# Eight key tiles are transposed and stored in the attention's last units instead of in the second value projection

## The chip, the cores and the metric

One NeuronCore of one Trainium2 chip runs the whole kernel. The metric is the device time of one execution in microseconds; lower is better. The engines are TensorE (PE in the rows), VectorE (DVE), ScalarE (ACT), GpSimd (POOL) and SyncE (SP), which here only issues DMAs.

## The reference

The kernel computes one inference step of a one-layer decoder for a prompt of 1024 tokens and 8 sampled tokens, each with a cache of 1024 positions in pages. Cut to what matters here:

```
h = rmsnorm(x); z = h @ w_in
gq, gk, gv, gr, g_lr, dq, dk, dv = split(z)
gla_o = chunked gated linear attention of gq, gk, gv
diff_o = (softmax(q1 k1^T) - lam * softmax(q2 k2^T)) @ v      # 4 heads, causal
x = x + concat(gla_o, diff_o) @ w_out
x = x + hier_moe(rmsnorm(x))                                   # 16 experts, top 2 of 4 in a group
return y, dk, dv, gla state                                    # dk of the prompt is an output: 1024 x 512
```

`dk` is the array that the change is about: the new keys are needed twice, with the head dimension on the partitions for the scores, and as rows by token, in float32, for the output `k_prompt`.

## The kernel before, in words

Every engine has a program of its own, written by hand in one order, and the engines meet at semaphores. Tokens go in tiles of 128 (NT = 8 tiles of the prompt, and a ninth of the 8 sampled tokens). PSUM has eight banks, `ps[:, 0]` to `ps[:, 7]`. The stages around the change are these, in order of time:

- **Key projection (DKG).** The keys are made transposed, as a high and a low float16 part, `kdh` and `kdl` (in `dg_reg`).
- **Second value projection (DVG).** PE makes the nine tiles of the values, 24 matmuls of 512 columns each (lines 2329 to 2331 of a shared helper, from `w_reg` and `hT_reg`), in banks 0 to 3. After each tile `between_values` runs `natural(n, t, hi, lo)`, eight matmuls against the identity that turn one tile of keys into rows by token in bank 4 or 5 (lines 2422 and 2423), and then one or two `value_quad(k)` (line 2548): a value quad multiplies four pages of the cached values, which SP has loaded into one of three buffers (`mix_reg`, or either half of `kv`), by the sampled tokens' weights. There are 16 quads, and 64 pages of 256 KB. SP reads each page's number from the page table (line 761) and then issues the load (line 762). ACT evicts each key tile to `knat` (line 1265, in `mix_reg`) and issues its store to `k_prompt` (line 1270); before the attention starts, ACT waits until all nine stores have landed (line 1274). The list `KNAT` puts the sampled tokens' keys first.
- **Attention.** UN = 32 units (8 tiles of queries times 4 heads, u = 0 to 31), followed by ten closing units u = 32 to 41 without scores of their own, in which the work behind the scores is finished. In unit u, PE transposes the combined weights (line 2633), multiplies by the values (line 2701), and does one quarter of an output product of an early tile (`early_product`, lines 2329 to 2331 from `w_reg` and `mix_reg`). `early_transpose(t, lo)` (line 2658, eight transposes into bank 4) puts one half of the normalised rows of tile t into bank 4, and ACT reads it away with line 1306 (`read_transposed`); PE may not write bank 4 again before that. `early_router` follows. ACT also squares the attention's output (line 1338), the new residual row (line 1289), rounds h2 (line 1354), and rounds the transposed attention output (line 649).
- **The product of tile 6** (`product(EARLY)`, 48 matmuls into banks 0 and 1) runs in unit 36, and the product of tile 7 (banks 2 and 3) after the closing units. Behind it come DVE's sum (line 2000), the norm, the router, and the experts. SP loads the first expert's weights when the stores of the early rows have landed and `s_h2T` says that tile 5 has been transposed:

```
            for i in range(2):
                sp.wait_ge(s_h2o[i], 16 * (EARLY // 2))
            sp.wait_ge(s_h2T, 2 * EARLY)
            load_gate_up(0)
```

Banks 2 and 3 hold scores up to unit 31 and nothing between that and the product of tile 7.

Of the kernel before, what the change touches and what calls it, by code (L numbers as in the profile page):

```python
# [98 lines left out]
KNAT = [NT] + list(range(NT))  # L99
# [62 lines left out]
def build(nc, I, O):  # L162
    ctx = ExitStack()
    with ctx:
# [125 lines left out]
        h2s = hT_reg[:, 4096:6144].bitcast(F16).rearrange("p (s d) -> p s d", s=2)  # L290
        h2T = hT_reg[:, 6144:8192].bitcast(F16).rearrange("p (s l k t) -> p s l k t", s=2, l=2, k=KC)
# [733 lines left out]
        def _(act):  # L1025
# [221 lines left out]
            for t in range(NT + 1):  # L1247
                r = rows(t)
                u = UNIT_AT[(DVG, t, 0)]
                if t in (3, 5):  # L1250
                    split_wo(t // 2 - 1)
                if t == NT - 1:
                    act.wait_ge(s_mT, NT + 1)
                    read_parts(DVG)
                if u % 2 == 0:
                    act.wait_ge(s_mm, u + 1)
                    act.activation(*plain_target(DVG, t, 0), ACT.Copy, scale=ISC2).then_inc(s_ev[BANK[u]], 1)
                v = KNAT[t]
                r = rows(v)
                act.wait_ge(s_kn, t + 2)  # L1260
                if t == 4:
                    act.wait_ge(s_dec, DEC["new_in"])
                if t >= 4:
                    act.wait_ge(s_kout[t % 4], 16 * (t // 4))
                act.activation(knat[0:r, t % 4], ps[0:r, 4 + (t + 1) % 2, :], ACT.Copy,
                               scale=1.0 / SC).then_inc(s_knr, 1)
                act.wait_ge(s_knr, t + 2)
                dst = O["k_prompt"][0, 0, v * P:(v + 1) * P].rearrange("p h e -> p (h e)") if v < NT \
                    else O["k_sample"][0, :, 0].rearrange("b h e -> b (h e)")
                act.dma_start(dst, knat[0:r, t % 4]).then_inc(s_kout[t % 4], 16)  # L1270
                if t == 4:
                    act.activation(dex, dex, ACT.Exp, scale=DK ** -0.5).then_inc(s_deca, 1)
            for i in range(4):
                act.wait_ge(s_kout[i], 16 * (NT // 4 + (i == 0)))
# [33 lines left out]
            for u in range(UN + 10):  # L1308
# [37 lines left out]
                if u % H == 1 and 0 <= (u - 17) // H < EARLY:  # L1346
                    t = (u - 17) // H
                    act.wait_ge(s_h2, t + 1)
                    if t == 0:
                        act.wait_ge(s_wol, KC // 2)  # L1350
                    if t >= 2:
                        act.wait_ge(s_h2o[t % 2], 16 * (t // 2))
                        act.wait_ge(s_h2T, 2 * (t - 1))
                    act.activation(h2se[:, t % 2, 0:D], h2e, ACT.Copy).then_inc(s_h2h, 1)
                if u == DEC_AT:
# [18 lines left out]

            for t in range(EARLY, NT + 2):
# [139 lines left out]
        def _(dve):  # L1515
# [502 lines left out]

            for t in range(EARLY, NT + 3):
# [306 lines left out]
        def _(pe):  # L2326
# [88 lines left out]
            def natural(n, t, hi, lo):  # L2415

                r = rows(t)
                if n >= 2:
                    pe.wait_ge(s_knr, n - 1)
                for h in range(H):  # L2420
                    out = ps[0:r, 4 + n % 2, P * h:P * h + P]
# [150 lines left out]
            def between_values(t, _):  # L2572
                natural(t + 1, KNAT[t], kdh, kdl)
                for k in QUADS_AT[t]:
                    value_quad(k)
# [42 lines left out]
            pe.wait_ge(s_knr, NT + 2)  # L2618
# [53 lines left out]
            for u in range(UN + 10):  # L2672
# [50 lines left out]
                if u % H == 1 and 0 <= (u - 21) // H < EARLY:  # L2723
                    early_router((u - 21) // H)
                if u == UN + 4:
                    product(EARLY)

            for t in range(EARLY + 1, NT + 3):
                if t == NT - 1:
                    product(t)  # L2730
# [210 lines left out]
```

## Time and profile before

| what | us |
|---|---|
| median of 3 runs | 917.7 (916.82 to 920.81) |
| the profiled execution, its own time | 914.89 |
| its span | 913.1 |
| PE busy in it | 788.1 (86%) |
| ACT busy in it | 444.9 (49%) |
| DVE busy in it | 561.8 (62%) |
| mean DMA rate over the span | 169 GB/s |

The difference of the last two times, 1.8 us, lies outside the span. All times of the rows below are from the span's start. A row of the timeline gives an instruction's start, its duration, the engine and the line; a matmul's duration is longer than the distance to the next one, since they are pipelined. `x8` means that eight alike were merged. In brackets stands for how long the engine was idle before, and what released it.

### The profile page before, as it was taken

How to read it: one execution, taken by the hardware profiler on the slowest of the kernel's cores; microseconds unless marked ns; L12 is line 12 of the kernel's file. 1: busy time of each engine (PE TensorE's matmuls, PEld its weight loads, DVE VectorE, ACT ScalarE, POOL GpSimd, SP SyncE). 2: the span in 40 equal slices, each digit the busy share in tenths (PEclk: the TensorE clock that was granted, in tenths of full speed). 3: DMA queues.
4: the chain of work that ended last, by engine and by line, in shares of the span. 5: the costliest groups of instructions: out<-in, count | busy, mean ns of one | idle time of the engine just before them, and what ended most of it. 6: DMA issues, size and time to landing. Idle time of an engine off the chain costs nothing. (4 is left out here: it accounts for less than half of the span.)

```text
span 913.1 us, 16430 instructions
## 1 busy us (share of the span) xinstructions
PE 788.1 (86%) x6255; PEld 494.6 (54%) x6255; DVE 561.8 (62%) x921; ACT 444.9 (49%) x855; POOL 249.2 (27%) x170
## 2 busy tenths in 40 slices
PE   3999979959899989976999998882389999998785
PEld 2766634335546644423566665441277787676551
DVE  6643569775444632248688875245675677787748
ACT  5432012557662412236467675234435757777733
POOL 2112987721134000002001000000424453532204
PEclk8999989979999999997999999986579999999998
DMA  9415795501031368881011101153596989999864
GB/s 310 102 50 151 234 300 183 194 0 47 1 99 47 93 224 256 258 279 69 25 70 70 71 24 47 47 209 129 190 312 222 293 259 302 304 338 342 233 207 186
DMA packets 98691, 154.70 MB, mean 169 GB/s; under 512 B 13573, under 2 KB 63301, under 8 KB 98610
## 3 DMA queue, kind: packets, MB, share of 16 engines
q1 hardware_dynamic: 91266, 132.97, 43.8%
q0 software_dynamic: 5728, 16.94, 7.3%
q10 hardware_dynamic: 1616, 3.70, 1.1%
q8 instruction: 51, 0.84, 0.4%
q14 instruction: 30, 0.25, 0.1%
HBM read 128.97 MB, written 27.48 MB: 171 GB/s over the span
## 5 line engine op out<-in xcount | busy, mean ns | idle before, releaser
L912 POOL TENSOR_TENSOR kv<-kv,gt 128x1024 f32<-128x1024 f32 x32 | 80.6, 2540 | 50.3 <-DMA kv<-in_cache_k 50.2
L2329 PE MATMUL ps<-hT_reg,w_reg 128*128 128x344 f16 x288 | 90.1, 313 | 3.5 <-DVE hT_reg L1564 3.5
L2330 PE MATMUL ps<-hT_reg,w_reg 128*128 128x344 f16 x288 | 89.9, 312 | 0.0
L2331 PE MATMUL ps<-hT_reg,w_reg 128*128 128x344 f16 x288 | 89.9, 312 | 0.0
L940 POOL TENSOR_TENSOR rst<-rst,neghalf 128x1 f32<-128x1 f32 (+3 forms) x27 | 24.8, 918 | 225.9 <-DVE rst L1861 225.9
L980 POOL DMA_INDIRECT sum_scratch<-kv,dest x23 | 59.4, 2583 | 89.9 <-DMA sum_scratch<-kv,dest 78.3
L2329 PE MATMUL ps<-w_reg,hT_reg 128*128 128x512 f16 x192 | 73.1, 381 | 1.9 <-ACT kv L1161 1.9
L2330 PE MATMUL ps<-w_reg,hT_reg 128*128 128x512 f16 x192 | 73.0, 380 | 0.0
L2331 PE MATMUL ps<-w_reg,hT_reg 128*128 128x512 f16 x192 | 72.9, 380 | 0.0
L1880 DVE TENSOR_REDUCE mxs<-ps 128x1 f32<-128x640 f32 (+7 forms) x48 | 45.7, 952 | 29.9 <-PE ps L2688 29.8
L2329 PE MATMUL ps<-hT_reg,dg_reg 128*128 128x128 f16 (+5 forms) x256 | 54.1, 238 | 2.0 <-DVE hT_reg L2157 2.0
L1320 ACT ACTIVATE hT_reg<-ps,mxn 128x128 f32<-128x128 f32 (+7 forms) x64 | 47.2, 740 | 17.7 <-DVE mxn L1881 11.5
L2329 PE MATMUL ps<-hT_reg,mix_reg 128*128 128x128 f16 (+4 forms) x256 | 52.9, 236 | 3.0 <-DVE hT_reg L2157 3.0
L1605 DVE TENSOR_REDUCE gbc<-kv 128x16 f32<-128x1024 f32 x32 | 38.8, 1215 | 26.2 <-POOL kv L912 26.2
L2330 PE MATMUL ps<-hT_reg,dg_reg 128*128 128x128 f16 (+5 forms) x256 | 54.1, 237 | 0.0
L2330 PE MATMUL ps<-hT_reg,mix_reg 128*128 128x128 f16 (+4 forms) x256 | 52.9, 236 | 0.0
L2331 PE MATMUL ps<-hT_reg,mix_reg 128*128 128x128 f16 (+4 forms) x256 | 52.8, 235 | 0.0
L2329 PE MATMUL ps<-w_reg,mix_reg 128*128 128x512 f16 x128 | 51.0, 399 | 0.0
L2331 PE MATMUL ps<-w_reg,mix_reg 128*128 128x512 f16 x128 | 50.7, 396 | 0.0
L2330 PE MATMUL ps<-w_reg,mix_reg 128*128 128x512 f16 x128 | 50.6, 396 | 0.0
L1298 ACT ACTIVATE hT_reg<-ps 128x512 f32<-128x512 f32 (+3 forms) x48 | 23.5, 489 | 45.0 <-PE ps L2633 44.1
L1579 DVE TENSOR_SCALAR dg_reg<-ps 128x512 f32<-128x512 f32 (+2 forms) x16 | 9.9, 616 | 54.7 <-PE ps L2331 45.0
(429 smaller groups left out, 2085.6 us busy)
## 6 DMA issues: line engine op xcount, KB each, us to landing
kv<-in_cache_k SPq DMA_DIRECT2D x64, 256.0 KB, 3.4
w_reg<-in_w_gate SPq DMA_DIRECT2D x16, 1024.0 KB
w_reg<-in_w_up SPq DMA_DIRECT2D x16, 1024.0 KB
w_reg<-in_w_down SPq DMA_DIRECT2D x16, 1024.0 KB, 14.8
w_reg<-in_w_in SPq DMA_DIRECT2D x12, 1024.0 KB, 6.6
mix_reg<-in_cache_v SPq DMA_DIRECT2D x32, 256.0 KB, 3.0
kv<-in_cache_v SPq DMA_DIRECT2D x32, 256.0 KB, 3.0
mix_reg<-in_x_prompt SPq DMA_DIRECT2D x8, 512.0 KB, 8.5
```

What stands on the lines that cost most here:

```text
L912: pool.tensor_tensor(pg, pg, qbc[:, b % 2].unsqueeze(1).to_broadcast([P, 2, 512]), ALU.mult).then_inc(s_kq, 1)
L940: pool.tensor_tensor(rst[pr, cr], rst[pr, cr], neghalf[pr, cr], ALU.pow).then_inc(s_rs, 1)
L980: pool.indirect_dma_start(out=sumd[:, :], out_offset=bass.IndirectOffsetOnAxis(ap=dest[0:r, 2 * e + g:2 * e + g + 1], axis=0), in_=yb[0:r, ...
L1298: act.activation(wT[:, v % 2, 4 * f:4 * f + w], ps[:, 4, 0:P * w].rearrange("p (j q) -> p j q", j=w), ACT.Copy).then_inc(s_wTe, 1)
L1320: act.activation(prob[:, u % 3, m, 0:n], scores(u, m), ACT.Exp, scale=DK ** -0.5 * ISC2, bias=mxn[:, u % 2, m:m + 1], accum_out=rsum[:, i ...
L1579: dve.tensor_scalar(*plain_target(g, blk, j), plain_scale(g, blk), None, ALU.mult).then_inc(s_ev[BANK[u]], 1)
L1605: dve.tensor_reduce(dsc[:, b, 2 * s:2 * s + 2], kv4[:, s].rearrange("p (g m d) -> p g m d", g=2, m=8), AX, ALU.add).then_inc(s_kh, 1)
L1880: link(dve.tensor_reduce(mxs[:, u % 2, ms], sc, AX, ALU.max))
L2329: pe.matmul(out, lh, rh, start=start, stop=False)
L2330: pe.matmul(out, lh, rl, start=False, stop=False)
L2331: return pe.matmul(out, ll, rh, start=False, stop=stop)
```

## The change

The eight prompt tiles' `natural` calls leave the second value projection and go to the end of the closing units u = 32 to 39, one in each, behind that unit's other PE work; the sampled tokens' call stays. They write banks 2 and 3. ACT's eviction and the store that follows go to the end of ACT's part of the same units; the eviction writes `keys_out`, a part of `hT_reg` that held attention weights and is used again for h2 afterwards. ACT waits for the stores to land before the loop that writes h2 there, not before the attention. PE waits that the keys are read before the product of tile 7, and DVE that they are transposed before it writes `x1` over `kdh` and `kdl`.

```diff
@@ ACT, second value projection
-                v = KNAT[t]
-                act.wait_ge(s_kn, t + 2)
+                if t == 0:
+                    act.wait_ge(s_kn, 2)
+                    act.activation(knat[0:NB, 0], ps[0:NB, 5, :], ACT.Copy, scale=1.0 / SC).then_inc(s_knr, 1)
+                    act.wait_ge(s_knr, 2)
+                    act.dma_start(O["k_sample"][0, :, 0].rearrange("b h e -> b (h e)"), knat[0:NB, 0]
+                                  ).then_inc(s_kout[0], 16)
                 if t == 4:
                     act.wait_ge(s_dec, DEC["new_in"])
-                if t >= 4:
-                    act.wait_ge(s_kout[t % 4], 16 * (t // 4))
-                act.activation(knat[0:r, t % 4], ps[0:r, 4 + (t + 1) % 2, :], ACT.Copy,
-                               scale=1.0 / SC).then_inc(s_knr, 1)
-                act.wait_ge(s_knr, t + 2)
...
-                act.dma_start(dst, knat[0:r, t % 4]).then_inc(s_kout[t % 4], 16)
...
-            for i in range(4):
-                act.wait_ge(s_kout[i], 16 * (NT // 4 + (i == 0)))
+            act.wait_ge(s_kout[0], 16)
@@ ACT, attention loop, end of unit u
+                if 0 <= u - UN < NT:
+                    t = u - UN
+                    act.wait_ge(s_kn, t + 3)
+                    if t >= 4:
+                        act.wait_ge(s_kout[t % 4], 16 * (1 + (t == 4)))
+                    act.activation(keys_out[:, t % 4], ps[:, 2 + t % 2, :], ACT.Copy, scale=1.0 / SC).then_inc(s_knr, 1)
+                    act.wait_ge(s_knr, t + 3)
+                    act.dma_start(O["k_prompt"][0, 0, t * P:(t + 1) * P].rearrange("p h e -> p (h e)"),
+                                  keys_out[:, t % 4]).then_inc(s_kout[t % 4], 16)
@@ ACT, before the loop over the last tiles
+            for i in range(4):
+                act.wait_ge(s_kout[i], 16 * (2 + (i == 0)))
@@ DVE, at the same place
+            dve.wait_ge(s_kn, NT + 2)
@@ PE
-            def natural(n, t, hi, lo):
+            def natural(n, t, hi, lo, bank=4):
...
-                    pe.wait_ge(s_knr, n - 1)
+                    pe.wait_ge(s_knr, n - 1 if n > 3 else 2)
...
-                natural(t + 1, KNAT[t], kdh, kdl)
+                if t == 0:
+                    natural(1, NT, kdh, kdl)
...
-            pe.wait_ge(s_knr, NT + 2)
+            pe.wait_ge(s_knr, 2)
@@ PE, attention loop, end of unit u, ahead of the product of tile 6
+                if 0 <= u - UN < NT:
+                    pe.wait_ge(s_p, 2 * UN)
+                    natural(u - UN + 2, u - UN, kdh, kdl, 2)
@@ PE, before the product of tile 7
+                    pe.wait_ge(s_knr, NT + 2)
```

In the changed kernel the lines are shifted: before's 2422 and 2423 are 2427 and 2428, 2658 is 2664, 2548 is 2553, 1306 is 1299, 1338 is 1331, 1289 is 1282, 1354 is 1347, and the keys' eviction and store are 1353 and 1355.

PE in the second value projection, at the end of one value tile; before:

```order
L2330 MATMUL ps<-w_reg,hT_reg 128x512
L2331 MATMUL ps<-w_reg,hT_reg 128x512
L2422 MATMUL ps<-ident,dg_reg 128x128
L2423 MATMUL ps<-ident,dg_reg 128x128
...
L2548 MATMUL ps<-kv,gbc 8x512 x4
L2329 MATMUL ps<-w_reg,hT_reg 128x512
```

and now:

```order
L2335 MATMUL ps<-w_reg,hT_reg 128x512
L2336 MATMUL ps<-w_reg,hT_reg 128x512
L2553 MATMUL ps<-kv,gbc 8x512 x4
L2334 MATMUL ps<-w_reg,hT_reg 128x512
L2335 MATMUL ps<-w_reg,hT_reg 128x512
```

The eight identity matmuls between the value tile and the value quad are gone, here and at seven more such places.

ACT in the closing units, from the squares of unit 35 on; before:

```order
L649 ACTIVATE mix_reg<-ps 128x4x128
L1338 ACTIVATE junk,ss<-ps,rinv 128x128 x2
L1289 ACTIVATE junk,ss<-kv 128x1024
L1306 ACTIVATE kv<-ps 128x1024
L1338 ACTIVATE junk,ss<-ps,rinv 128x128 x2
L1306 ACTIVATE kv<-ps 128x1024
```

and now:

```order
L649 ACTIVATE mix_reg<-ps 128x4x128
L1353 ACTIVATE hT_reg<-ps 128x512
L1355 DMA out_k_prompt<-hT_reg 128x512
L1331 ACTIVATE junk,ss<-ps,rinv 128x128 x2
L1282 ACTIVATE junk,ss<-kv 128x1024
L1353 ACTIVATE hT_reg<-ps 128x512
L1355 DMA out_k_prompt<-hT_reg 128x512
L1299 ACTIVATE kv<-ps 128x1024
L1331 ACTIVATE junk,ss<-ps,rinv 128x128 x2
L1353 ACTIVATE hT_reg<-ps 128x512
L1355 DMA out_k_prompt<-hT_reg 128x512
L1299 ACTIVATE kv<-ps 128x1024
```

An eviction and an issue of the keys now stand ahead of each of ACT's reads of the transposed h2.

PE at the same place, from the end of tile 5's output product to the product of tile 6; before:

```order
L2330 MATMUL ps<-w_reg,mix_reg 128x512
L2331 MATMUL ps<-w_reg,mix_reg 128x512
L2658 MATMUL ps<-ident,w_reg 128x128 x16
L2329 MATMUL ps<-w_reg,mix_reg 128x512
L2330 MATMUL ps<-w_reg,mix_reg 128x512
```

and now:

```order
L2336 MATMUL ps<-w_reg,mix_reg 128x512
L2427 MATMUL ps<-ident,dg_reg 128x128
L2428 MATMUL ps<-ident,dg_reg 128x128
...
L2664 MATMUL ps<-ident,w_reg 128x128 x8
L2427 MATMUL ps<-ident,dg_reg 128x128
...
L2664 MATMUL ps<-ident,w_reg 128x128 x8
L2427 MATMUL ps<-ident,dg_reg 128x128
...
L2334 MATMUL ps<-w_reg,mix_reg 128x512
```

Three of the moved key tiles stand around the two halves of h2's transposition of tile 4.

## Rows read from the trace of the kernel before

**Rows 1.** The page's head: the span.

```profile
span 913.1 us, 16430 instructions
```

**Rows 2.** Timeline of PE in the second value projection.

```profile
345.18 0.22 PE L2422 MATMUL ps<-ident,dg_reg 128*128 128x128 f16 x1
...
345.72 1.04 PE L2548 MATMUL ps<-kv,gbc 128*8 128x512 f32 x8
...
354.23 1.04 PE L2548 MATMUL ps<-mix_reg,gbc 128*8 128x512 f32 x8 [0.75 <-DMA mix_reg<-in_cache_v]
...
396.26 1.04 PE L2548 MATMUL ps<-mix_reg,gbc 128*8 128x512 f32 x8 [1.43 <-DMA mix_reg<-in_cache_v]
```

**Rows 3.** Timeline of SP's queue in the same stage: single issues of pages.

```profile
337.33 0.33 SPq L762 DMA_DIRECT2D kv<-in_cache_v  x1
...
347.55 1.04 SPq L762 DMA_DIRECT2D mix_reg<-in_cache_v  x1
...
362.90 0.33 SPq L762 DMA_DIRECT2D mix_reg<-in_cache_v  x1
364.64 0.33 SPq L762 DMA_DIRECT2D mix_reg<-in_cache_v  x1
...
392.43 0.33 SPq L762 DMA_DIRECT2D mix_reg<-in_cache_v  x1
```

**Rows 4.** Lines 761 and 762 over the whole span, ns (landing in us): minimum, median, maximum.

```profile
L761 SPq TENSOR_LOAD <-ptab x64: 262/268/920, 295.0 to 391.7; - x64
...
DMA to landing us min/median/max: 2.4/3.0/4.4
```

**Rows 5.** Timeline of ACT in the stage, with the issues of its queue (ACTq).

```profile
346.50 0.37 ACTq L1270 DMA_DIRECT2D out_k_prompt<-mix_reg  x1
...
352.54 0.60 ACT L1265 ACTIVATE mix_reg<-ps 128x512 f32<-128x512 f32 x1 [6.07 <-PE ps L2423]
...
353.63 1.91 ACT L1244 ACTIVATE w_reg<-w_reg 128x2048 f16<-128x2048 f32 x1 [0.49 <-ACT mix_reg L1265]
...
399.28 0.37 ACT L1320 ACTIVATE hT_reg<-ps,mxn 128x128 f32<-128x128 f32 x1 [4.79 <-DMA out_k_prompt<-mix_reg]
```

**Rows 6.** Timeline of PE at the attention's start.

```profile
399.78 1.88 PE L2710 MATMUL ps<-kv,lsel 128*8 128x512 f32 x4 [1.49 <-DVE kv L1943]
```

**Rows 7.** Timeline of PE in the closing units.

```profile
563.87 0.61 PE L2658 MATMUL ps<-ident,w_reg 128*128 128x128 f16 x8
565.79 0.63 PE L2633 MATMUL ps<-ident,hT_reg 128*128 128x128 f32 x4 [1.31 <-ACT kv L1306]
...
576.57 0.61 PE L2658 MATMUL ps<-ident,w_reg 128*128 128x128 f16 x8
579.88 0.61 PE L2658 MATMUL ps<-ident,w_reg 128*128 128x128 f16 x8 [2.70 <-ACT kv L1306]
...
596.51 0.61 PE L2658 MATMUL ps<-ident,w_reg 128*128 128x128 f16 x8 [1.31 <-ACT kv L1306]
```

**Rows 8.** Timeline of ACT in the closing units.

```profile
564.51 1.02 ACT L1306 ACTIVATE kv<-ps 128x1024 f16<-128x1024 f16 x1 [1.74 <-PE ps L2658]
...
577.57 1.06 ACT L1289 ACTIVATE junk<-kv 128x1024 f32<-128x1024 f32 x1 [2.10 <-DVE kv L1889]
...
578.62 1.00 ACT L1306 ACTIVATE kv<-ps 128x1024 f16<-128x1024 f16 x1
579.53 0.36 ACT L1338 ACTIVATE junk<-ps,rinv 128x128 f32<-128x128 f32 x1
...
580.52 1.02 ACT L1306 ACTIVATE kv<-ps 128x1024 f16<-128x1024 f16 x1 [0.20 <-PE ps L2658]
```

**Rows 9.** The chain that ended last, around the product of tile 7.

```profile
594.56 2.94 DMA h_scratch<-w_reg
...
612.06 1.29 DVE dg_reg L2000 x2
```

**Rows 10.** One window: length, busy time of PE, PEld, DVE, ACT, POOL, then granted clock, DMA share, GB/s.

```profile
600.00:620.00 20.00, 17.02 (x117) 7.29 (x115) 8.34 (x11) 8.76 (x12) 1.10 (x2) 0.88 0.45 160
```

More of the change, by code:

```diff
@@ L98 @@
 KCH = 4 * NB
-KNAT = [NT] + list(range(NT))
 VQ = 2 * NPG
@@ L290, in build @@
         h2s = hT_reg[:, 4096:6144].bitcast(F16).rearrange("p (s d) -> p s d", s=2)
+        keys_out = hT_reg[:, 4096:6144].rearrange("p (s c) -> p s c", s=4)
         h2T = hT_reg[:, 6144:8192].bitcast(F16).rearrange("p (s l k t) -> p s l k t", s=2, l=2, k=KC)
@@ L1257, in _ @@
                     act.activation(*plain_target(DVG, t, 0), ACT.Copy, scale=ISC2).then_inc(s_ev[BANK[u]], 1)
-                v = KNAT[t]
-                r = rows(v)
-                act.wait_ge(s_kn, t + 2)
+                if t == 0:
[4 more added lines that the diff above has]
+                                  ).then_inc(s_kout[0], 16)
                 if t == 4:
                     act.wait_ge(s_dec, DEC["new_in"])
-                if t >= 4:
-                    act.wait_ge(s_kout[t % 4], 16 * (t // 4))
-                act.activation(knat[0:r, t % 4], ps[0:r, 4 + (t + 1) % 2, :], ACT.Copy,
-                               scale=1.0 / SC).then_inc(s_knr, 1)
-                act.wait_ge(s_knr, t + 2)
-                dst = O["k_prompt"][0, 0, v * P:(v + 1) * P].rearrange("p h e -> p (h e)") if v < NT \
-                    else O["k_sample"][0, :, 0].rearrange("b h e -> b (h e)")
-                act.dma_start(dst, knat[0:r, t % 4]).then_inc(s_kout[t % 4], 16)
-                if t == 4:
                     act.activation(dex, dex, ACT.Exp, scale=DK ** -0.5).then_inc(s_deca, 1)
-            for i in range(4):
-                act.wait_ge(s_kout[i], 16 * (NT // 4 + (i == 0)))
+            act.wait_ge(s_kout[0], 16)
             squared = [0, 0]
@@ L2413, in next_x @@
                     x_transpose(t)
-            def natural(n, t, hi, lo):
+            def natural(n, t, hi, lo, bank=4):
                 r = rows(t)
                 if n >= 2:
-                    pe.wait_ge(s_knr, n - 1)
+                    pe.wait_ge(s_knr, n - 1 if n > 3 else 2)
                 for h in range(H):
-                    out = ps[0:r, 4 + n % 2, P * h:P * h + P]
+                    out = ps[0:r, bank + n % 2, P * h:P * h + P]
                     pe.matmul(out, hi[:, h, span(t)], ident16[:], start=True, stop=False)
```

## The prediction

> **What bounds the kernel now.** The page's head gives the span, 913.1 us [rows 1]; the profiled execution's own time is 914.89, and the median of the runs is 917.7, so 2.8 lies between my base and the number to be forecast. PE is busy for 86% of the span, but what the change is worth is decided at two places, and I read each by its timelines: first who waits, then for what.
>
> In the second value projection PE looks like the bound: it runs without a break but for three short waits, and each wait is for pages of cached values. Two stand in [rows 2], 0.75 us at 354.23 and 1.43 at 396.26, the last value quad, behind which the attention begins. So two chains end there almost together, PE's and SP's. SP issues the 48 pages of quads 4 to 15 from 337.33 to 392.43 [rows 3]; most of the 47 distances are 1.08 to 1.13 us, of which only 0.33 is the issue; the median read of the page number is 0.27 [rows 4] and the rest of the 1.09 is register work. 47 x 1.09 is 51.2, the rows give 55.1: 3.9 us are stalls. Two stand in [rows 3]: the issue at 347.55 took 1.04 instead of 0.33, and between 362.90 and 364.64 lies 1.74 instead of 1.09, for a page-number read that took up to 920 ns [rows 4]. In no place is SP held by PE: each buffer had been freed before SP asked.
>
> In the closing units PE is the bound, and wherever it stops it stops for ACT's read of bank 4: 1.31 at 565.79, 2.70 at 579.88, 1.31 at 596.51 [rows 7]. There ACT is the second half of a serial chain, not a spare engine.
>
> **Step 1, what leaves the value projection.** One call of `natural` is eight matmuls, and PE spends from 345.18 to 345.62 on it: 0.44 us (345.72 less the 0.10 before a quad) [rows 2]. Eight of them are 3.5 us. By PE alone that would be the gain. But the last quad starts when its pages land, 396.26, 1.43 us after PE was ready. If SP's stream stays as it is, PE only waits 3.5 us longer, and the gain is nothing, or at most 0.8: the last page took 3.8 us from its issue at 392.43 to 396.26, against a median of 3.0 [rows 3, 4], and one key store was on its way beside it.
>
> If the stalls go with the stores, the stream ends earlier. The first of the eight stores is issued at 346.50 [rows 5]; the stalled page issue at 347.55 begins 1.05 behind it. Each of the five long stalls of the stream follows a store by 0.9 to 1.7 us, and ahead of the first store there is only a short one of 0.36. The five sum to about 3.0. I take them as caused by the stores. Then the last page is issued at 389.5 and lands at 392.5 to 393.3. PE, freed of 3.5 us and of most of the wait at 354.23, is ready at about 390.7, so the pages still end the stage. Gain: 396.26 less 392.9, **3.3 us** (bounds 0 and 4.2, the second being 3.5 plus the 0.75 wait).
>
> The Trainium skill (Perfetto Trace Analysis, DMA Instruction — HWDGE) says that the block which writes the descriptors is shared by the issuing sequencers and locked, and that the reported issue includes the wait for the lock. By that rule eight stores of some 0.36 us could take at most 2.9 from SP. The stalled issue agrees; the long page-number reads are not explained by it.
>
> **Step 2, the wait ahead of the attention.** ACT's first exponential waits for the last store until 399.28 [rows 5]. That wait goes. It is worth nothing: PE has 1.88 us of work from 399.78 on that waits for DVE [rows 6], and it hides the exponentials. At no cover it would be 0.6.
>
> **Step 3, unit 32 to 33.** From here on all is the cost. In the rows of before PE's transposes at 563.87 end their turn at 564.31. Now `natural` follows, to 564.75, its last result some 0.2 later, and ACT, in its own order, has to evict the keys before it may read bank 4. What an eviction with its store costs ACT: 352.54 to 353.63, **1.09 us** [rows 5] (activation 0.60, then the issue, 0.37, for which ACT waits on its own result). So the read that began at 564.51 [rows 8] begins at 566.03, and PE goes on at 567.31 instead of 565.79: **+1.5**. Nothing hides it; PE is the stage's bound.
>
> **Step 4, units 33 to 36.** The key tiles of units 33 and 34 add 0.44 each to PE: transposition of tile 4 starts at +2.40, 578.97 instead of 576.57 [rows 7]. Before, ACT came to its read of the first half at 578.62, behind the square at 577.57 [rows 8]. Now it evicts tile 2 (579.2 to 580.26), does unit 35's two squares (579.53 to 580.32, 0.8) and the row's square (577.57 to 578.62, 1.05) to 582.15 [rows 8], evicts tile 3 (to 583.22), reads bank 4 (1.26 to PE's start, as from 578.62 to 579.88), and PE's second half starts at 584.48 instead of 579.88: **+4.6**, 2.2 more. Behind it stands tile 4's 0.44: the product of tile 6 starts at **+5.0**. ACT's keys of units 36 and 37 lie beside that product, 12 us, and cost nothing.
>
> **Step 5, units 37 to 41.** Counted from T, the start of tile 7's transposes (592.97 before, 3.54 ahead of the row at 596.51), PE does tile 5 (0.44), the transposes, tile 6 and, after DVE's h2 part, which arrives when it did before, the first half of tile 5's h2 at T + 1.62, then key tile 7. ACT has the keys at T + 0.67, its rounding at T + 1.73, then two evictions in a row, T + 2.22 to T + 4.35, and only then the read of bank 4, which before began at T + 2.26. So PE's second half comes at T + 5.62 instead of T + 3.54 (596.51 [rows 7]): **+2.1** for the product of tile 7. The same +2.1 stops `s_h2T`, which now releases the first expert's load: before, the store of 594.56 landed at 597.5 and released it [rows 9], now the transposes do, 1.65 later. Both meet at DVE's sum at 612.06 [rows 9]: about **+1.8** there. The cost is 5.0 + 1.8 = **6.8 us**. Its bounds: if the issue were free to ACT (0.49 an eviction, the distance of two activations), the same sum gives 4.5; if a store's landing held ACT once (3.7 us after the last issue at T + 3.95, ahead of ACT's next work at T + 9.8) nothing is added.
>
> **Step 6, the clock.** The window from 600 to 620 shows a granted clock of 0.88 [rows 10]: a stretch at the lower level, 1.2 instead of 2.4 GHz, follows the idle time of the closing units, and there is a shorter one behind the 2.70 idle at 579.88. The change makes two idle times longer, 1.31 to 2.6 and 2.70 to 4.6. Whether the first now brings a stretch at the low level of its own is open. The window's 12% of 20 us, twice, is a stretch of 4.8 us and cost half of it, 2.4; I take such a cost at less than even chance, **+0.9**. The bounds are 0 and +4.8, two more of them.
>
> The sum is 6.8 - 3.3 + 0.9 = **+4.4**: 919.3 in the profile's terms, 922.1 beside the median.
>
> **Rivals.** (a) SP's stalls are not the stores' doing and the stream ends as before. For it: three of the eight stores have no long stall behind them. The gain is 0 to 0.8: +6.9 to +7.7, 924.6 to 925.4. (b) The kernel is not slower, because the key matmuls keep PE active in the gaps: both low stretches go, the one in [rows 10], 2.4, and the one behind 579.88, at most as much. It gives 6.8 - 3.3 - 4.8 = -1.3, 916.4. It decides if the products of tiles 6 and 7 run every matmul at the full clock. Against it: a key tile fills 0.44 while the gap it stands in grows by 1.3 or more. The Trainium skill (TensorE: Matmul & The Clock Gate, HAM oscillation) holds that idle gaps bring the low clock back; longer gaps speak against this change by it. (c) The clock costs one stretch more, 2.4, or two: 6.8 - 3.3 + 2.4 = +5.9, 923.6, up to 926.0. (d) ACT's cost is the lower one: 4.5 - 3.3 + 0.9 = +2.1, 919.8.
>
> **How the numbers follow.** My forecast has 0.43, (a) 0.25, (b) 0.10, (c) 0.10, (d) 0.12. About 0.5%, 4.6 us, is what a measurement of this kernel can tell from no change, so the line is 922.3. Half of the forecast's own spread, 920 to 924, lies over it: slower by more is 0.21 + 0.25 + 0.10 = 0.56 less a little of (a), 0.53; faster by more than 0.5% is half of (b), 0.05; the rest, 0.42, is between. The range leaves out most of (b), the bottom of (d) and the top of (c): 918.8 to 926.0.
>
> **What would show it.** In the changed trace: the distances of SP's page issues all near 1.09 and the last quad before 393.5 (step 1; near 396 means (a)). PE's wait for bank 4 of 2.6 us at unit 33, 4.6 at unit 36 and about 3.1 and 1.5 in units 40 and 41, the excess each time taken by ACT's 1353 with 1.09 from its start to the next activation. The sum of step 4, read from value projection's end to the product of tile 6, is wrong if ACT got to the keys in a time when it had nothing else. The forecast fails if PE's low-clock stretches move by more than one, or if the experts' loads, which now start later, meet other traffic.

## The result, and the profile after

The changed kernel takes 924.1 us (median of 7 runs, 921.21 to 928.12) against 917.7 (7 runs, 914.2 to 920.81) on the same chip: a ratio of 1.0084, 95% interval 1.0055 to 1.0114. Slower, by 6.4 us in the medians; +4.4 was forecast. The ratio on record is not the quotient of the two medians (1.0070); here and below it leaves out runs in a slower state, among them one of e (3882.9 us) and one of f (1058.3). By it the change costs 7.7 us, with an interval of 5.0 to 10.5, and the forecast's 4.4 lies just under that interval. The profiled execution has its own time of 921.7 and this span, which answers to [rows 1]:

```profile
span 919.9 us, 16438 instructions
```

6.8 us more than before. I follow the two traces from front to back.

**Ahead of the stream.** The stream of pages begins 2.0 us later than in [rows 3], at 339.33. This has no part in the change: up to there both kernels run the same instructions. A window of the changed one shows a granted clock of 0.83 (length, busy time of PE, PEld, DVE, ACT, POOL, clock, DMA share, GB/s) where the same work before ran at 1.00; that is 0.5 us of it, and the other 1.5 come in between 195 and 199 us. The second trace of the changed kernel (h, below) begins its stream at 336.77, earlier than before. So the 2.0 are one execution's chance, and below I count from the stream's start.

```profile
160.00:170.00 10.00, 8.04 (x48) 2.81 (x46) 8.20 (x10) 0.60 (x1) 6.67 (x3) 0.83 0.81 259
```

**The value projection.** SP's first and last page issue of quads 4 to 15, and the reads of page numbers over the span (minimum, median, maximum in ns), to be held against [rows 3, 4]:

```profile
339.33 0.33 SPq L762 DMA_DIRECT2D kv<-in_cache_v  x1
...
391.47 0.33 SPq L762 DMA_DIRECT2D mix_reg<-in_cache_v  x1
```

```profile
L761 SPq TENSOR_LOAD <-ptab x64: 264/268/288, 297.0 to 390.8; - x64
```

The stream is 52.14 long instead of 55.10, and the longest read of a page number is 288 ns, not 920: the stalls are gone with the stores. PE's timeline at the end of the stage and the start of the attention ([rows 2, 6]):

```profile
394.96 1.04 PE L2553 MATMUL ps<-mix_reg,gbc 128*8 128x512 f32 x8 [2.60 <-DMA mix_reg<-in_cache_v]
398.48 3.58 PE L2716 MATMUL ps<-kv,lsel 128*8 128x512 f32 x4 [1.32 <-DVE kv L1947]
```

The last quad starts 55.63 us after the stream instead of 58.93: the 3.3 us of the forecast. But PE now waits 2.60 for its pages instead of 1.43, and the four matmuls of the second row take 3.58 instead of 1.88. Two windows from the last quad to unit 19's early transposes, the same work in both kernels, show what came of that:

```profile
396.26:475.65 79.39, 67.13 (x460) 36.95 (x461) 61.22 (x142) 45.17 (x137) 9.20 (x9) 0.94 0.27 99
```

```profile
394.96:476.19 81.23, 69.55 (x460) 37.52 (x461) 61.22 (x142) 45.18 (x137) 9.20 (x9) 0.89 0.26 94
```

The first is before, the second after: 1.84 us longer at a clock of 0.89 instead of 0.94. More than half of the 3.3 is lost again there. The lower clock falls right behind the last quad; again before, then after:

```profile
396.00:404.00 8.00, 5.36 (x48) 1.97 (x48) 4.55 (x15) 2.70 (x13) 0.00 (x0) 1.00 1.04 363
```

```profile
396.00:404.00 8.00, 6.36 (x38) 1.80 (x37) 3.89 (x14) 2.30 (x12) 0.00 (x0) 0.57 1.00 348
```

**The closing units**, PE's timeline, to be held against [rows 7]:

```profile
567.82 0.63 PE L2639 MATMUL ps<-ident,hT_reg 128*128 128x128 f32 x4 [2.35 <-ACT kv L1299]
...
585.01 1.01 PE L2664 MATMUL ps<-ident,w_reg 128*128 128x128 f16 x8 [4.50 <-ACT kv L1299]
...
603.72 0.61 PE L2664 MATMUL ps<-ident,w_reg 128*128 128x128 f16 x8 [2.89 <-ACT kv L1299]
```

The waits for bank 4 grew from 1.31, 2.70 and 1.31 to 2.35, 4.50 and 2.89. ACT's timeline shows what stands in front of its read of bank 4, which ends them. For the wait of 4.50 it is tile 3's eviction and its issue, and tile 2's was ahead of them:

```profile
582.69 0.58 ACT L1353 ACTIVATE hT_reg<-ps 128x512 f32<-128x512 f32 x1
583.30 0.34 ACTq L1355 DMA_DIRECT2D out_k_prompt<-hT_reg  x1
583.74 1.02 ACT L1299 ACTIVATE kv<-ps 128x1024 f16<-128x1024 f16 x1 [0.47 <-ACT hT_reg L1353]
```

and for the wait of 2.89:

```profile
600.31 0.59 ACT L1353 ACTIVATE hT_reg<-ps 128x512 f32<-128x512 f32 x1
600.93 0.34 ACTq L1355 DMA_DIRECT2D out_k_prompt<-hT_reg  x1
601.37 0.60 ACT L1353 ACTIVATE hT_reg<-ps 128x512 f32<-128x512 f32 x1 [0.47 <-ACT hT_reg L1353]
602.00 0.34 ACTq L1355 DMA_DIRECT2D out_k_prompt<-hT_reg  x1
602.44 1.02 ACT L1299 ACTIVATE kv<-ps 128x1024 f16<-128x1024 f16 x1 [0.47 <-ACT hT_reg L1353]
```

Two evictions, 1.06 us from start to start, then the read of bank 4 that PE waits for. The chain that ended last goes on from there ([rows 9]):

```profile
603.72 0.62 PE ps L2664 x8
604.41 0.38 SPq L781
604.84 10.81 DMA w_reg<-in_w_up
615.68 1.92 ACT dg_reg L1370
617.65 2.17 issue
619.83 1.29 DVE dg_reg L2004 x2
```

DVE's sum, line 2004 now, starts at 619.83 instead of 612.06. Of these 7.77 us 0.54 had come in before unit 32; 7.2 are the closing units' and the load's. Behind it the routing, at a lower clock for somewhat longer than before, adds about 1.0, and the experts give 1.9 back. Neither needs the change as its cause: from DVE's sum to the end all twelve traces of this document have the same work, and take 298.9 (f) to 304.1 us (g) for it. So 2.0 - 3.3 + 1.8 + 7.2 + 1.0 - 1.9 = 6.8, the difference of the spans.

### The profile page after: what moved, and what is told of

Its sections match the earlier page's. It is cut to its first block and busy times, and to the rows that moved or that the text cites. A ratio compares the mean times of both kernels' runs of the same rounds, so it can differ in the third digit from the quotient of the medians.

```text
span 919.9 us, 16438 instructions
## 1 busy us (share of the span) xinstructions
PE 794.0 (86%) x6255; PEld 497.1 (54%) x6255; DVE 561.7 (61%) x921; ACT 445.2 (48%) x855; POOL 252.4 (27%) x170
## 5 line engine op out<-in xcount | busy, mean ns | idle before, releaser
L980 POOL DMA_INDIRECT sum_scratch<-kv,dest x23 | 61.8, 2686 | 86.9 <-DMA sum_scratch<-kv,dest 75.4
L2334 PE MATMUL ps<-w_reg,mix_reg 128*128 128x512 f16 x128 | 50.4, 394 | 0.0
L2335 PE MATMUL ps<-w_reg,mix_reg 128*128 128x512 f16 x128 | 50.1, 391 | 0.0
L2336 PE MATMUL ps<-w_reg,mix_reg 128*128 128x512 f16 x128 | 49.9, 390 | 0.0
```

What stands on the lines that cost most here:

```text
L980: pool.indirect_dma_start(out=sumd[:, :], out_offset=bass.IndirectOffsetOnAxis(ap=dest[0:r, 2 * e + g:2 * e + g + 1], axis=0), in_=yb[0:r, ...
L2334: pe.matmul(out, lh, rh, start=start, stop=False)
L2335: pe.matmul(out, lh, rl, start=False, stop=False)
L2336: return pe.matmul(out, ll, rh, start=False, stop=stop)
```

## The experiments

Ten runs were made, one of them the changed kernel once more. Three questions were open: did the stores cause SP's stalls; is the closing units' cost ACT's evictions and nothing else; and what do the pieces give by themselves, so that a better place can be found. Ratios are to the kernel before on the same chip, with 95% intervals; they differ from the quotients of the medians by up to 0.25%. The code cuts show the lines that matter and leave out the semaphore waits that go with them. The columns behind come from each run's profiled execution: the length of SP's stream of quads 4 to 15; the time from the last quad to unit 19's early transposes with the granted clock of that window; the time from unit 32's early transposes to the product of tile 7.

| kernel | median us | ratio | stream | last quad to unit 19, clock | closing units |
|---|---|---|---|---|---|
| before | 917.7 | | 55.10 | 79.39, 0.94 | 35.19 |
| changed | 924.1 | 1.0084 [1.0055, 1.0114] | 52.14 | 81.23, 0.89 | 41.86 |
| a_no_stores | 914.71 | 0.9961 [0.9936, 0.9987] | 53.44 | 79.39, 0.94 | 35.20 |
| b_no_transposes | 915.66 | 0.9994 [0.9961, 1.0027] | 57.23 | 83.49, 0.87 | 33.51 |
| c_no_keys | 912.26 | 0.9947 [0.9917, 0.9978] | 52.99 | 79.94, 0.89 | 35.20 |
| d_no_issue | 919.4 | 1.0034 [1.0009, 1.0058] | 53.88 | 80.63, 0.92 | 40.73 |
| e_late_reads | 917.9 | 1.0013 [0.9985, 1.0041] | 52.38 | 81.52, 0.90 | 34.29 |
| f_first_units | 916.72 | 0.9991 [0.9970, 1.0011] | 52.48 | 83.23, 0.90 | 35.20 |
| g_pe_only | 915.66 | 0.9987 [0.9961, 1.0014] | 52.26 | 81.21, 0.89 | 34.38 |
| h_changed_again | 926.32 | 1.0110 [1.0077, 1.0143] | 52.54 | 82.62, 0.88 | 45.39 |
| i_late_no_stores | 912.04 | 0.9941 [0.9921, 0.9962] | 52.53 | 81.65, 0.90 | 34.00 |
| j_split_places | 915.9 | 0.9989 [0.9965, 1.0013] | 52.24 | 81.83, 0.92 | 34.21 |

a to d shared a chip (before: 916.1), e to h another (916.02), i and j a third (917.92).

### a_no_stores: the kernel before without the eight stores

```
                 act.activation(knat[0:r, t % 4], ps[0:r, 4 + (t + 1) % 2, :], ...)
-                act.wait_ge(s_knr, t + 2)
-                act.dma_start(dst, knat[0:r, t % 4]).then_inc(s_kout[t % 4], 16)
+                if t == 0:
+                    act.wait_ge(s_knr, 2)
+                    act.dma_start(dst, knat[0:r, 0]).then_inc(s_kout[0], 16)
```

> The kernel before, with the eight stores of the prompt's keys left out (k_prompt is not written; transposes and evictions stay). My theory: the stores cause SP's long stalls, so the stream of the 48 pages of quads 4 to 15 takes about 52 us from the first issue to the last instead of 55.1, and as PE still has its 3.5 us of key transposes, PE and pages end together: the last value quad comes 2.5 to 3.0 us earlier against the stage's start, and the whole is about 2.5 faster than before, less what the clock takes. Rival (a): the stream still takes 55 and the last quad is where it was; no change in time.

SP's reads of page numbers are at most 281 ns:

```profile
L761 SPq TENSOR_LOAD <-ptab x64: 263/268/281, 298.1 to 393.1; - x64
```

The stream shrinks by 1.7, and PE, which still makes the transposes, waits no more than 0.2 for the last quad. The stage's gain from the stores alone is 2.0 (56.89 from the stream's start to the last quad instead of 58.93), because PE is then the bound; I had expected 2.5 to 3.0, and a stream of 52 instead of 53.44. The whole is 3.6 us faster by the ratio, and its interval holds the 2.5 expected.

### b_no_transposes: the kernel before without PE's transposes, stores kept

```
             def between_values(t, _):
-                natural(t + 1, KNAT[t], kdh, kdl)
+                if t == 0:
+                    natural(1, NT, kdh, kdl)
```

ACT's eight evictions are left out too; it stores what the slots hold.

> The kernel before, with PE's and ACT's work on the eight prompt key tiles left out and the eight stores kept (they store what is in the buffer, so k_prompt is wrong). My theory: the stores still stall SP, the stream takes 55 us, the last quad starts when its pages land as before, and PE merely waits 3 to 4.5 us for it instead of 1.43; no gain (within 1 us). Rival (PE is the stage's bound): the last quad comes 3.5 us earlier, 3.5 faster.

The stream is not shorter but 2.1 longer: seven reads of a page number took 640 to 1164 ns, each 1.0 to 1.6 us behind the issue of a store. The row of line 761, and one page's issue, 2.65 us behind the first store:

```profile
L761 SPq TENSOR_LOAD <-ptab x64: 263/268/1164, 294.2 to 392.7; - x64
```

```profile
347.21 1.33 SPq L762 DMA_DIRECT2D mix_reg<-in_cache_v  x1
```

So PE's 3.5 us are worth nothing while the stores stay, as step 1 had it; and with PE idle for 4.26 us ahead of the last quad, the attention's start ran at a clock of 0.52:

```profile
397.92 1.90 PE L2549 MATMUL ps<-mix_reg,gbc 128*8 128x512 f32 x8 [4.26 <-DMA mix_reg<-in_cache_v]
```

```profile
396.00:404.00 8.00, 4.86 (x26) 1.10 (x27) 2.92 (x9) 1.62 (x8) 0.00 (x0) 0.52 0.94 321
```

### c_no_keys: the changed kernel without the eight key tiles

```
-                if 0 <= u - UN < NT:
-                    pe.wait_ge(s_p, 2 * UN)
-                    natural(u - UN + 2, u - UN, kdh, kdl, 2)
```

and ACT's part, so that the prompt's keys are missing from the output.

> The changed kernel with the eight prompt key tiles left out altogether (k_prompt is not written). It is the change's gain alone. My theory: the stage's end comes 3.3 us earlier as in the changed kernel, the closing units are as in before, the low-clock stretch at the attention's start costs about 1.8 of it: 1.5 to 3.3 faster than before, and 7 to 8 faster than the changed kernel. Rival: the closing units' delay comes from the earlier start or the clock and not from the keys; then it stays within 2 us of the changed kernel.

0.9947, 4.9 us by the ratio: this is what taking the tiles out of the value projection is worth if they cost nothing elsewhere. That is more than the 1.5 to 3.3 expected, though the interval, 2.0 to 7.6 us, reaches into it. The closing units are those of before to 0.01 us. The changed kernel's 1.0084 to 1.0110 lies 1.4 to 1.6% above it, 12.5 to 15 us, where I had expected 7 to 8; the profiled spans (910.1 and 919.9, less the 2.7 us by which the stream begins later in the changed trace) show 7.1. The rival, less than 2, is out by either.

### d_no_issue: the changed kernel, evictions kept, stores left out

```
                     act.activation(keys_out[:, t % 4], ps[:, 2 + t % 2, :], ...)
-                    act.wait_ge(s_knr, t + 3)
-                    act.dma_start(O["k_prompt"]..., keys_out[:, t % 4]).then_inc(s_kout[t % 4], 16)
```

> The changed kernel with the stores left out, transposes and evictions in the closing units kept (k_prompt is not written). My theory: an eviction then costs ACT 0.5 instead of 1.09 us. PE's idle time before the row that waits for bank 4 in unit 33 falls from 2.35 to about 1.8, in unit 36 from 4.50 to about 3.3, in unit 40 from 2.89 to about 1.2, and the load of the first expert's weights is released about 3.3 us earlier relative to unit 32: 2.5 to 3.5 us faster than the changed kernel, still 2 to 4 slower than before. Rival: the issue costs nothing, the evictions alone make the delay; same as the changed kernel.

```profile
564.50 0.63 PE L2632 MATMUL ps<-ident,hT_reg 128*128 128x128 f32 x4 [1.80 <-ACT kv L1299]
580.50 1.01 PE L2657 MATMUL ps<-ident,w_reg 128*128 128x128 f16 x8 [3.31 <-ACT kv L1299]
```

The waits are 1.80 and 3.31, as expected, and 1.80 at the third place, where I expected 1.2. Without ACT's part altogether (g, below) they are 0.86, 1.81 and 0.87; so at the first two places the eviction alone adds 0.94 and 1.50, and the issue with its wait 0.55 and 1.19 more. Up to the product of tile 6 the time is 20.52 instead of 22.26, 1.7 less. The closing units as a whole shrink by only 1.1, though, because a stretch at the lower clock, from 579.56 on, made that product 1.6 longer, 12.24 instead of 10.67 (0.91 between 560 and 600). The kernel is 0.34% slower than before, as expected, and 0.5 to 0.8% faster than the changed one, 4.6 to 7 us where I had expected 2.5 to 3.5.

### g_pe_only: the changed kernel, only PE's transposes kept

```
-                    pe.wait_ge(s_knr, n - 1 if n > 3 else 2)
+                    pe.wait_ge(s_knr, n - 1 if n < 2 else 2)
```

and ACT's part of the eight tiles taken out whole.

> The changed kernel with PE's transposes in the closing units kept, and ACT's evictions and stores left out (k_prompt is not written). My theory: PE's eight tiles cost 0.44 each only where PE would not have waited for ACT: units 33, 34 and 37, and part of 38: 1.3 to 2 us over the kernel with no keys at all. The idle times for bank 4 are 0.9 in unit 33, 2.3 in 36 and 0.9 in 40. Rival: it costs 3.5 or more, the most of the changed kernel's delay.

Without ACT's eight evictions and stores the closing units take 34.38, 0.8 less than before the change although PE does more:

```profile
565.46 0.63 PE L2628 MATMUL ps<-ident,hT_reg 128*128 128x128 f32 x4 [0.86 <-ACT kv L1299]
579.97 0.61 PE L2653 MATMUL ps<-ident,w_reg 128*128 128x128 f16 x8 [1.81 <-ACT kv L1299]
```

The matmuls fill part of the waits for bank 4 (0.86 instead of 1.31, 1.81 instead of 2.70), but not for nothing. From unit 32's early transposes to the product of tile 6, at the full clock in both traces, it takes 17.32 here and 16.45 before: PE's part costs 0.9. In the changed kernel the same work takes 22.26, so most of the cost is on ACT.

What more than pays for the 0.9 is the clock on that product, 10.14 from its first matmul to its last against 11.83 before, where a stretch at the lower level begins behind the wait of 2.70. That the key matmuls keep this stretch away is not shown: b's closing units are those of before, with the same wait of 2.70, and its product takes 10.15 at the full clock. The windows on that product, before and b:

```profile
580.00:584.50 4.50, 4.50 (x20) 1.89 (x19) 2.22 (x7) 2.29 (x4) 1.02 (x1) 0.62 0.02 4
```

```profile
586.00:597.00 11.00, 11.00 (x76) 5.34 (x74) 1.98 (x7) 2.05 (x3) 1.02 (x1) 1.00 0.00 0
```

The kernel is yet not as fast as c: 0.9987, intervals that overlap. I had expected 1.3 to 2 us between them; by the ratios it is 3.7. In the traces the two differ by only 0.1 us from the stream's start to DVE's sum; 3.1 us of g's longer span lie behind the sum, where both have the same work.

### h_changed_again: the changed kernel once more

> The changed kernel once more, unaltered, beside these. Expected: 5 to 9 us slower than before, with the same idle times for bank 4 (2.35, 4.50, 2.89) and a page stream of about 52 us; whether a low-clock stretch falls on the attention's start may differ.

The waits are the same to 0.01 us (2.35, 4.50, 2.88), but in this execution low-clock stretches began at 567.44 and 584.51, the first right behind the wait of 2.35 at unit 33, which the first trace had passed at the full clock. Windows of this kernel and of the first trace of the changed one:

```profile
566.00:572.00 6.00, 5.20 (x29) 4.74 (x30) 0.90 (x4) 1.82 (x4) 0.00 (x0) 0.72 0.12 43
```

```profile
566.00:572.00 6.00, 4.18 (x31) 3.40 (x32) 1.29 (x5) 3.01 (x5) 0.55 (x1) 1.00 0.12 45
```

The closing units took 45.39 instead of 41.86: 3.5 us, between two executions of one program. From the stream's start on, this trace stands 10.6 us behind that of the kernel before, the first one 4.8. The ratio, 1.0110, is 10.1 us, a little over the 5 to 9 expected.

### e_late_reads: complete, ACT evicts only where it stood idle

```
+KEYS_MADE_AT = (32, 33, 34, 35, 37, 38, 39, 40)
+KEYS_READ_AT = {33: (0,), 34: (1,), 36: (2, 3), 38: (4,), 40: (5,), 41: (6, 7)}
...
-                if 0 <= u - UN < NT:
-                    t = u - UN
+                for t in KEYS_READ_AT.get(u, ()):
```

> The changed kernel, complete, with the same work in another order: ACT evicts the key tiles only where it had idle time (tile 0 at the end of unit 33, 1 in 34, 2 and 3 in 36 behind the read of bank 4, 4 in 38, 5 in 40, 6 and 7 in 41), and PE makes tiles 4 to 7 behind the product of tile 6. My theory: the delay of the closing units comes from evictions that stand ahead of ACT's reads of bank 4. The idle time in unit 33 is then 0.9 (1.31 less the key tile), in unit 36 about 2.3, and the closing units cost 1 to 2.5 us instead of 7; 4 to 6 faster than the changed kernel and within 2 of before. Rival: it is PE's own eight key tiles and the clock; then at most 2 faster than the changed kernel.

```profile
563.44 0.63 PE L2643 MATMUL ps<-ident,hT_reg 128*128 128x128 f32 x4 [0.86 <-ACT kv L1301]
577.95 0.61 PE L2668 MATMUL ps<-ident,w_reg 128*128 128x128 f16 x8 [1.81 <-ACT kv L1301]
593.27 0.61 PE L2668 MATMUL ps<-ident,w_reg 128*128 128x128 f16 x8 [0.99 <-ACT kv L1301]
...
613.67 0.61 PE L2353 MATMUL ps<-zer 128*128 128x512 f16 x1 [6.01 <-DVE mix_reg L2033]
```

The closing units cost nothing now, 34.29, though here too without the low stretch on the product of tile 6 (10.14). But a wait of 6.01 us stands behind the products, so that from unit 32's early transposes to DVE's sum it takes 50.72 against 48.19 before. By the ratios the kernel is 6.5 to 9 us faster than the changed one, more than the 4 to 6 expected, and level with before. The chain names a transfer:

```profile
594.43 13.63 DMA w_reg<-in_w_up
```

13.63 us instead of 9.91. Four stores, 1 MB, are issued between 591.6 and 596.5, into the same time as two tiles of x and the first expert's weights. That was a guess from this trace; i tests it.

### i_late_no_stores: e without the stores of tiles 4 to 7

```
-                    act.dma_start(O["k_prompt"]..., keys_out[:, t % 4]).then_inc(s_kout[t % 4], 16)
+                    if t < 4:
+                        act.dma_start(O["k_prompt"]..., keys_out[:, t % 4]).then_inc(s_kout[t % 4], 16)
```

> The kernel of the run before it with late reads, with one thing left out: the stores of prompt key tiles 4 to 7 (1 MB) are not issued, so those 1024 rows of keys are missing from the output; their transposes and ScalarE's four evictions stay. Question: what was the new idle of 6.01 us of TensorE between the products and the routing? Theory: the transfers. With late reads the four stores are issued between 591 and 597 us, in the midst of the two tiles of x and of w_gate and w_up, and the DMA engines are busy from 590 to 607 without a break at about 350 GB/s; 1 MB is 2.9 us of that. Then w_up lands about 3 us sooner, the idle is 3 us (2.5 to 3.5), and the kernel is 2.5 to 3 us shorter than with late reads, at about 915. Rival: the idle is not the transfers' but comes from ScalarE's four evictions late in its queue, ahead of tile 6's h2: then it stays 5 to 6 us and the time 917 to 918.

```profile
595.47 9.87 DMA w_reg<-in_w_up
```

```profile
610.95 0.46 PE L2354 MATMUL ps<-zer 128*128 128x512 f16 x1 [2.49 <-DVE mix_reg L2034]
```

The load takes 9.87 again, and PE's wait is 2.49 instead of 6.01, at the end of the 2.5 to 3.5 expected. (The 350 GB/s of the expectation were too many: e's window from 590 to 607 has 309, by which 1 MB is 3.4 us, nearer to the 3.5 and 3.8 by which the wait and the load shrank.) From unit 32's early transposes to DVE's sum it takes 46.91. The evictions are the same, so the stores' traffic was the cause. The median, 912.04, is better than the 915 I expected, and 0.9941 is level with c: with keys read late and no late store, the place is free.

### f_first_units: complete, keys made in attention units 1 to 8

```
-                if 0 <= u - UN < NT:
-                    pe.wait_ge(s_p, 2 * UN)
-                    natural(u - UN + 2, u - UN, kdh, kdl, 2)
+                if 1 <= u <= NT:
+                    natural(u + 1, u - 1, kdh, kdl, 5)
```

ACT evicts to `knat`, SP issues the stores.

> The keys, complete, in the attention's first units 1 to 8 instead of the closing ones: PE makes one tile at the end of each unit in bank 5, ACT evicts it to knat in the same unit, and SP, which has nothing to do there, issues the stores. PE, ACT and DVE wait for each other there anyway. My theory: the value projection gains as in the changed kernel (last quad 3.3 us earlier against the stream's start), the closing units are as in before, and the first units lose 0 to 3 us: 5 to 7 faster than the changed kernel and 0 to 4 faster than before. Rival: ACT is the bound of the first units and each eviction costs its 0.5 us in full, or the stores meet the loads of w_out; then no faster than before.

The closing units are those of before again, 35.20 with waits of 1.31 and 2.70. From the last quad to unit 19 it takes 83.23: 1.7 more than e at the same clock of 0.90, and 3.8 more than before, where I had expected 0 to 3. That eats the stream's gain.

### j_split_places: complete, tiles 0 to 3 in units 1 to 4, the rest in units 32 to 35

```
+                if 1 <= u <= 4:
+                    natural(u + 1, u - 1, kdh, kdl, 5)
...
+KEYS_MADE_AT = (32, 33, 34, 35)
+KEYS_READ_AT = {33: (4,), 34: (5,), 36: (6, 7)}
```

> Complete. Tiles 0 to 3 of the prompt's keys are made in the attention's units 1 to 4 (bank 5, evicted to the old slots, stored by SyncE), tiles 4 to 7 in units 32 to 35 of the closing units, read by ScalarE where it stood idle there (units 33, 34 and 36), so that no store is issued after about 580 us. Theory: the closing units cost nothing against before (waits for bank 4 of at most 1.9 us, product of tile 7 34.3 us after tile 7's first transposes), the loads of w_gate and w_up meet no store, so the new idle of the run with late reads is 3 us at most, and the first units cost about 1.1 us, half of what eight tiles cost there. The stream's 3.3 us stay gained, the clock's loss of 1.8 at the attention's start stays too: about 1 to 2 us under the kernel before, ratio 0.998, which five rounds may not tell from none. Rival: the loads are late even without stores because the products end sooner than the loads can (the same idle of 6 us as before); then as with late reads, 1.001.

Each part did as expected: closing units 34.21, and behind the products PE waits 0.30 where e had 6.01:

```profile
612.17 0.39 PE L2361 MATMUL ps<-zer 128*128 128x512 f16 x1 [0.30 <-DVE mix_reg L2041]
```

The four tiles in the first units cost 1.2 against d, which has the same clock of 0.92 there. The median is 915.9, 2.0 under before, but the interval of the ratio, 0.9965 to 1.0013, holds 1. These runs don't tell it from no change; no complete version was shown faster than the kernel before.

## Why the prediction was right, and where its sizes were off

**Step 1, the gain of 3.3:** right, 58.93 to 55.63. That the stores stall SP and not PE's transposes is shown from both sides: without the stores there the longest read of a page number is 281, 283, 367 and 282 ns in a, c, d and h; with the stores and without PE's part (b) there are seven long ones. Rival (a) falls. Not all of the five stalls are the stores', though. Single page issues of 0.65 to 1.28 us remain in a, c and d, and the stream without stores varies from 52.1 to 53.9. The stalled issue that step 1 began with, at 347.55, stands 10.2 us behind the stream's start, and without any store one of 0.53 to 1.11 us stands at 10.2 to 10.3 in a, d, f, g and h. That it followed a store by 1.05 us proves nothing. The four long reads are the stores', 2.3 of the 3.0 us. The Trainium skill (Perfetto Trace Analysis, DMA Instruction — HWDGE) has the wait for the lock on the descriptor writer inside the reported issue; here the stores' stall stands in the read of the page number ahead of the issue, so the lock's accounting doesn't cover it. In that section the Trainium skill names the sequencers of VectorE and SyncE as those that share the writer. That ScalarE's stores take the same lock was my step, and no run here shows it.

**Step 2, worth nothing:** right. The wait for the last store ahead of the attention is gone, and PE's four matmuls still start 3.52 us behind the last quad (399.78 - 396.26 before, 398.48 - 394.96 now). In a, where that wait is gone too and the clock is that of before, the time to unit 19 is 79.39 as before.

**Steps 3 to 5, the closing units:** right in place and nearly in size. Each number here is the start in the changed trace less the start before, less the 0.54 from before unit 32. Unit 33: 567.82 - 565.79 - 0.54 = 1.5, forecast 1.5. Tile 4's second half: 585.01 - 579.88 - 0.54 = 4.6, forecast 4.6. The product of tile 6 began 5.8 later, not 5.0 (586.67 - 580.32 - 0.54), because the transposes and the key tile behind the wait ran at the lower clock (1.01 for the eight instead of 0.61); the product itself was then 1.2 shorter than before (10.67 and 11.83), since the stretch was nearly over. At unit 41 the second half of tile 5 stands at +6.7 (603.72 - 596.51 - 0.54), forecast 5.0 + 2.1 = 7.1. DVE's sum: 7.2, forecast 6.8. The remaining 0.4 hides two misses: step 5 had the sum gain on the product (1.8 for 2.1), while in truth the load of w_up took 10.81 instead of 9.91. The last key stores were on their way beside it, but that they did this is not shown: h has the same stores and 9.78, and the nine traces with no key store near the load have 9.18 to 10.53. In e the load took 13.63, far outside that, and i showed that those 3.7 are the stores'. The text named "other traffic" as a way to fail, without a price. Rival (d) falls: against g, the issue and its wait cost 0.55 at unit 33, where one key tile stands ahead of the read of bank 4, and 1.19 at unit 36, where two do.

**Step 6, the clock:** this is the term that was mis-sized, and looked for in one place only. +0.9 stood for one stretch at less than even chance in the closing units. The first trace has none more there; the second has one more, and together with the longer one behind it 3.5 us. That is rival (c), in some executions and not in others. And 1.8 us (3.2 in h) were lost between the last quad and unit 19, which no step priced, though step 1 had said that PE would be ready 2 us ahead of its pages. In the two kernels where PE still makes the transposes among the values and stands still for at most 1.43 us ahead of the last quad, before and a, that time is 79.39 at a clock of 0.94. In all others it is 79.94 to 83.49 at 0.87 to 0.92 (f and j also have key tiles there). In eight of these ten traces TensorE falls to 1.2 instead of 2.4 GHz at the last quad or within 2 us of it, in or behind a wait of 2.21 to 4.26 us. The other two, d and j, had waited 2.92 and 1.94 us and show no such stretch; they lose their time to a longer one later on (a clock of 0.83 from 420 to 440, before 0.91), and j to its key tiles. Their windows around the last quad, d first:

```profile
392.00:408.00 16.00, 10.28 (x82) 3.94 (x82) 10.06 (x31) 6.38 (x28) 2.20 (x3) 1.00 0.71 258
```

```profile
390.00:410.00 20.00, 14.12 (x124) 5.92 (x116) 10.86 (x32) 8.32 (x32) 2.31 (x3) 1.00 0.85 297
```

So it is not the length of that wait alone, and what decides it stays open. The Trainium skill (TensorE: Matmul & The Clock Gate, HAM oscillation) says that idle gaps bring the low clock back; the traces agree in direction, with d and j as exceptions, and I used the rule for the closing units only. Rival (b), a gain of the clock by key matmuls in the gaps, fails for the changed kernel. Its mechanism is neither shown nor ruled out: where the key matmuls fill the waits and ACT's part does not lengthen them (e, g, i, j), no low stretch falls on the product of tile 6, while before, a, c and f have one; but b, with no key matmuls there, has none either.

The whole, without the chance part ahead of the stream: -3.3 + 1.8 + 7.2 + 1.0 - 1.9 = +4.8 in the first trace, and in h, by the same places (the gain of the stream's stage, the way to unit 19, that to DVE's sum, the rest), -3.2 + 3.2 + 9.7 + 0.8 = +10.6 with rounding. The ratios say +7.7 and +10.1; +4.4 was forecast. So the forecast had the places and the direction right and was 3 to 6 us too small. That the first trace comes within 0.4 of it is luck: the 1.8 that no step priced is partly made up by the 0.9 of chance behind the sum. What was missing is the clock, 1.8 and 3.2 at the attention's start against nothing, and up to 3.5 between two executions in the closing units against +0.9. I can't split it further. Also open in part is why c (0.9947) and g (0.9987) differ: in the traces it is time behind DVE's sum, but one trace each doesn't tell for the other runs.

## What to carry to other kernels

Work taken off an engine that shares its end with a queue is worth only what the queue then gives, and the engine's new idle time can be charged by the clock behind it, as in eight of ten traces here: price the first stretch of work after the place you emptied. When you move work into an engine's gaps, look at every engine that touches it: TensorE's part here filled waits and cost 0.9 us, while ScalarE's 1.06 us per tile, set ahead of the read that TensorE waits for, cost nearly all the rest. And before you credit a matmul in a gap with keeping the clock up, look for a trace without it that has the same clock. And a store is also traffic: 1 MB put next to a load on the path made that load 3.7 us longer, so ask for each moved transfer what else is in flight.

## What the runs showed of the hardware

- A store from SBUF issued on ACT's queue made the next reads of a page number on SP's queue, ordinarily 0.27 us, take 0.64 to 1.16 us, with 0.9 to 1.7 us between the store's issue and the long read. The first seven of the eight prompt stores did so in b, four in before, and no run without stores there has a read over 0.42 us.
- ACT spends 0.34 to 0.37 on the issue itself, but 1.06 us pass from the eviction's start to the next activation, of which the activation is 0.60: it waits for its own result before the issue, and the next activation starts late behind it (the 0.47 in ACT's rows).
- The granted clock of the same work differs between executions of one program: 1.00 and 0.72 between 566 and 572 us.
- 1 MB of stores issued beside the load of w_up made that load 13.63 us long (e) instead of 9.87 (i). Without key stores near it the same load varies from 9.18 (b) to 10.53 (a).
